# Attention values kept in the array and weights normalised on GpSimd: one change to a two-block transformer kernel

## What is computed

```
u    = rms_norm(x, norm_pre);  proj = u @ w_in
q_a, kv_a, g_a, z_a, qkv_b, z_b, merge = split(proj)
# attention a: 8 heads of 64, three branches, each gated per head and token
o_a  = g[0] * softmax(q_a kc) vc  +  g[1] * softmax(q_a ks) vs  +  g[2] * softmax(q_a kw) vw
y_a  = o_a * silu(z_a)
o_b  = softmax(q_b k_b) v_b            # attention b, 8 heads, no gate
y_b  = o_b * silu(z_b)
m    = sigmoid(gate_a) * (y_a @ w_a) + sigmoid(gate_b) * (y_b @ w_b)
x    = x + rms_norm(m @ w_o, norm_post)
```

## Time and profile before

| what | us |
|---|---|
| median of 3 runs | 634.45 |
| lowest and highest | 634.45, 637.77 |
| span of the profiled execution, first to last instruction | 632.1 |
| own time of the profiled execution | not listed apart from the runs; span and surroundings are taken as the median's 634.45, so 2.35 lie around the span |
| PE busy, 3510 matmul instructions | 568.5 |
| DVE busy, 701 instructions | 298.7 |
| ACT busy, 453 instructions | 213.9 |
| POOL busy, 68 instructions | 38.9 |
| DMA | 193.36 MB, mean 306 GB/s |

### The profile page before, as it was taken

One profiled execution on the slowest core, in us unless ns is written; L12 is line 12 of the kernel. 1 busy time (PEld: TensorE's weight loads), 2 busy tenths in 40 slices (PEclk: granted clock), 3 DMA queues, 4 the chain that ended last, 5 costly groups with the idle time before them and its releaser, 6 DMA issues.

```text
span 632.1 us, 8828 instructions
## 1 busy us (share of the span) xinstructions
PE 568.5 (90%) x3510; PEld 372.4 (59%) x3510; DVE 298.7 (47%) x701; ACT 213.9 (34%) x453; POOL 38.9 (6%) x68
## 2 busy tenths in 40 slices
PE   8999999999999999999998999999989765675685
PEld 7988977777867887868774444455443411321232
DVE  2556467675668977774747766234220100100002
ACT  3345443654523622665337754131110100100002
POOL 2000000000000000010004433000000000000000
PEclk9999999999999999999999999999999997897899
DMA  9984965659679887435658333768999999999994
GB/s 358 331 284 166 378 272 199 255 227 383 268 311 432 321 302 290 173 113 234 245 242 336 163 101 134 311 244 324 399 430 427 425 428 426 428 423 431 426 419 175
DMA packets 23069, 193.36 MB, mean 306 GB/s; under 512 B 4211, under 2 KB 5619, under 8 KB 11253
## 3 DMA queue, kind: packets, MB, share of 16 engines
q1 hardware_dynamic: 21732, 190.11, 75.4%
q0 software_dynamic: 288, 1.57, 0.6%
q10 hardware_dynamic: 1008, 1.12, 0.6%
HBM read 191.21 MB, written 1.06 MB: 304 GB/s over the span
## 4 chain that ended last, share of the span: by engine, by line
PE 65%; DMA 20%; DVE 6%; ACT 3%; SPq 2%; issue 1%; POOL 1%; ACTq 0%; POOLq 0%; DVEq 0%
PE bank L1240 27%; DMA ring<-in_stream 19%; PE bank L1904 6%; PE bank L1217 5%; PE bank L1228 5%; PE bank L1840 2%; PE bank L1286 2%; PE bank L1768 2%; PE bank L1703 2%; PE bank L1555 2%; PE bank L1826 2%; SPq L833 2%; PE bank L1616 1%; PE bank L1950 1%; PE bank L1662 1%
## 5 line engine op out<-in xcount | busy, mean ns | idle before, releaser
L1240 PE MATMUL bank<-weight_parts,u_parts 128*128 128x512 f32 (+1 forms) x384 | 116.5, 386 | 0.8 <-DVE weight_parts L2216 0.4
L1240 PEld LDWEIGHTS bank<-weight_parts,u_parts 128*128 128x128 f32 x384 | 69.9, 188 | 17.0 <-issue 2.7
L2216 DVE TENSOR_TENSOR weight_parts<-ring,weight_parts 128x1024 fp32r<-128x1024 f32 x56 | 66.5, 1222 | 23.9 <-ACT weight_parts L859 21.9
L859 ACT ACTIVATE weight_parts<-ring 128x1024 fp32r<-128x1024 f32 x56 | 57.2, 1055 | 14.5 <-PE bank L1240 14.1
L1240 PE MATMUL bank<-weight_parts,x_parts 128*128 128x512 f32 (+1 forms) x128 | 48.4, 378 | 0.0
L1240 PE MATMUL bank<-u_parts,weight_parts 128*128 128x256 f32 x192 | 36.5, 286 | 0.9 <-DVE weight_parts L2216 0.7
L1193 POOL TENSOR_TENSOR small<-small 128x1 f32<-128x1 f32 (+1 forms) x14 | 8.5, 608 | 417.8 <-DVE small L2649 200.0
L921 ACT ACTIVATE sp<-sp,small 128x128 f32<-128x128 f32 (+1 forms) x48 | 21.3, 444 | 32.0 <-DVE small L2125 32.0
L1240 PEld LDWEIGHTS bank<-u_parts,weight_parts 128*128 128x128 f32 x192 | 30.4, 191 | 2.4 <-issue 1.2
L1141 ACT ACTIVATE sp<-bank 128x512 f32<-128x512 f32 x4 | 2.4, 597 | 74.1 <-PE bank L1904 74.1
L2621 DVE SCALAR_TENSOR_TENSOR sp<-sp,bank 128x512 f32<-128x512 f32 x4 | 2.7, 685 | 52.2 <-ACT sp L1141 52.2
(11 more groups left out here) (367 smaller groups left out, 1064.1 us busy)
## 6 DMA issues: line engine op xcount, KB each, us to landing
ring<-in_stream SPq DMA_DIRECT2D x35, 2048.0 KB, 9.7
qk<-in_stream SPq DMA_DIRECT2D x9, 2048.0 KB, 12.5
parts<-in_stream SPq DMA_DIRECT2D x9, 2048.0 KB, 20.0
tabs<-in_stream SPq DMA_DIRECT2D x6, 2048.0 KB, 17.1
mo<-in_stream SPq DMA_DIRECT2D x5, 2048.0 KB, 26.9
vvc<-in_stream SPq DMA_DIRECT2D x5, 2048.0 KB, 30.0
ring<-in_stream SPq DMA_DIRECT2D x6, 1024.0 KB, 6.4
vvc<-in_vecs SPq DMA_DIRECT2D x12, 512.0 KB, 8.6
```

The lines of the kernel that those rows point to most:

```text
L859: ins = act.activation(dst, src, ACT.Copy, scale=scale)
L1240: ins = pe_.matmul(o, lhs(a, c, i), rhs(b, c, i), start=(c == 0 and n == 0), stop=(c == chunks - 1 and n == 2))
L2216: dve.tensor_tensor(quarter(low, name, q), quarter(slot(name), name, q), quarter(high, name, q).bitcast(F32), ALU.subtract).then_inc(split ...
```

## The change

- **POOL scales the weights p.** When a unit's exponentials are done, POOL takes `sums ** -1` (4 columns), for NSA and WIN multiplies by the gate (4 columns), and multiplies the unit's p in `sp` by them, four `tensor_scalar` of 128, 256, 128, 256 columns. `turn` on PE waits for that (`p_scaled`) in place of `exps`. The two DMA issues for the mask table stand between the units on POOL.
- **Value products turned.** p is now the moving operand, the values the stationary one: two matmuls of 256 and two of 128 columns, in pairs on half of the array's columns each. The output has features on partitions.
- **DVE's `unit_out`** becomes one operation of 128x256 (copy, add, or for MOBA the multiplication by silu(z_b), so the `yb` multiplication goes).
- **The groups `yaT0`, `yaT1`, `ybT0`, `ybT1` are gone.** ACT makes the high part of all 1024 columns in one operation, DVE the low part in one.
- **`za` and `zb` become `turned_products`** (48 matmuls of 256 columns in place of 24 of 512), and `cO` is computed turned, with as many matmuls as before.
- **`parts_product` goes by quarters**: for each quarter of the weights it does all outputs, and releases the quarter after them.

```
@@ DENSE @@
-         "cO0", "cO1", "gA00", "gA10", "yaT0", "gA01", "yaT1", "gA11", "modT0", "wa00", "ybT0",
-         "wa10", "ybT1", "wa01", "wa11", "gB00", "gB10", "cxT00", "cxT01", "cxT10", "cxT11",
+         "cO0", "cO1", "gA00", "gA10", "gA01", "gA11", "modT0", "wa00",
+         "wa10", "wa01", "wa11", "gB00", "gB10", "cxT00", "cxT01", "cxT10", "cxT11",
@@ schedule @@
-        if name == "cO1":
+        if name == "gA10":
             out.append(("ya", 0))
+        if name == "gA01":
+            out.append(("ya low", 0))
         if name == "gA11":
             out.append(("yb", 0))
+            out.append(("yb low", 0))
@@ ACT @@
+                elif kind in ("ya", "yb"):
+                    if kind == "ya":
+                        eng.wait_ge(ya_ready, 1)
+                    else:
+                        eng.wait_ge(outs, len(UNITS))
+                    high, full = ((yaT, oa), (ybT, ob))[kind == "yb"]
+                    copy(high, full, None, 0.5).then_inc(y_high, 1)
@@ POOL @@
+                    for u, (kind, j) in enumerate(UNITS):
+                        if u in (5, 7):
+                            i = (u - 5) // 2
+                            eng.wait_ge(masked, 6 + 2 * i)
+                            eng.dma_start(both[0][:, i::2], both[1][:, i::2]).then_inc(moba_table_in[i], 16)
+                        eng.wait_ge(exps, u + 1)
+                        pool.tensor_tensor(rc[:, u, :], sums[:, u, :], half[:, 3:4].to_broadcast([P, 4]), ALU.pow)\
+                            .then_inc(unit_recip_in, 1)
+                        eng.wait_ge(unit_recip_in, u + 1)
+                        if kind != MOBA:
+                            g0 = 8 * (kind + 1) + j
+                            pool.tensor_tensor(rc[:, u, :].rearrange("p (b q) -> p b q", b=2),
...
+                            eng.wait_ge(unit_recip_gated, u + 1)
+                        for b in range(2):
+                            for q in range(TOK):
+                                k = spn[:, u % 2, b, P * q:P + S * q]
+                                ins = pool.tensor_scalar(k, k, rc[:, u, 2 * b + q:2 * b + q + 1], None, ALU.mult)
+                        ins.then_inc(p_scaled, 1)
@@ PE, parts_product @@
-                for i, o in enumerate(outs_):
-                    for c in range(chunks):
-                        if not last and i == 0 and c % 2 == 0:
-                            eng.wait_ge(split_v, 4 * k + quarter + c // 2 + 1)
...
-                        if last and i == len(outs_) - 1 and c % 2 == 1 and c < chunks - 1:
-                            ins.then_inc(part_used, 1)
+                for c in range(0, chunks, 2):
+                    if not last:
+                        eng.wait_ge(split_v, 4 * k + quarter + c // 2 + 1)
+                    for i, o in enumerate(outs_):
+                        for d in (c, c + 1):
...
+                    if last and c < chunks - 2:
+                        ins.then_inc(part_used, 1)
@@ PE, turn and pv @@
-                    eng.wait_ge(exps, u + 1)
+                    eng.wait_ge(p_scaled, u + 1)
...
+                    for t, a in ((0, 0), (1, P)):
+                        for b in range(2):
+                            c = HD * b if typ != MOBA else HD * (2 * j + b)
+                            ins = pe_.matmul(VB[HD * b:HD * b + HD, a:S], v[:, t, c:c + HD],
+                                             ptn[:, u % 2, b, S * t:S * t + S - a], start=(t == 0), stop=(t == 1),
+                                             tile_position=(0, HD * b))
@@ DVE, unit_out, ya and the low parts @@
+                o = VB[:, 0:S]
+                if u == 8:
+                    kept(eng, "zb1")
+                if kind == NSA:
+                    ins = dve.tensor_copy(oa[:, j, :], o)
+                elif kind == WIN:
+                    ins = dve.tensor_tensor(oa[:, j, :], oa[:, j, :], o, ALU.add)
+                else:
+                    ins = dve.tensor_tensor(ob[:, j, :], zb[:, j, :], o, ALU.mult)
...
+                elif kind in ("ya low", "yb low"):
+                    which = kind[:2] == "yb"
+                    low, high, full = ((yalow, yaT, oa), (yblow, ybT, ob))[which]
+                    eng.wait_ge(y_high, 1 + which)
+                    dve.scalar_tensor_tensor(low, full, 0.5, high.bitcast(F32), ALU.mult, ALU.subtract).then_inc(y_low, 1)
```

More of the change, by code:

```diff
@@ L130 @@
 N_VEC = 16
-VEC_AFTER = {"wa10": [0], "ybT1": [1], "cxT11": [2, 3, 4, 5], "wb00": [6, 7], "mT00": [8, 9], "wo00": [10, 11, 12, 13], "cc0": [14, 15]}
+VEC_AFTER = {"wa00": [0], "wa10": [1], "cxT11": [2, 3, 4, 5], "wb00": [6, 7], "mT00": [8, 9], "wo00": [10, 11, 12, 13], "cc0": [14, 15]}
 VEC_LOADS = {"W9": [0, 1], "M7": [2, 3], "W11": [4, 5], "WO0": [6, 7, 8, 9], "C1": [10, 11], "WO1": [12, 13, 14, 15]}
@@ L1355, in dense @@
                     done(turned_products(name, "W1", 256 * i, i == 1), name)
[L1356 removed]
+                elif name[:2] in ("za", "zb"):
+                    i = int(name[2])
+                    begin(name)
+                    done(turned_products(name, {"za": "W6", "zb": "W7"}[name[:2]], 256 * i, i == 1), name)
+                elif name[:2] in ("va", "vb", "gA", "gB"):
                     t = int(name[2])
[L1358 removed]
+                    sl = {"va": "W2", "vb": "W5", "gA": "W8", "gB": "W10"}[name[:2]]
                     if name[:2] in ("gA", "gB") and name[3] == "1":
@@ L1417, in dense @@
                     if (t, h) == (0, 0):
-                        for i in range(2):
-                            kept(eng, f"y{name[1]}T{i}")
+                        eng.wait_ge(y_low, 1 + (name[1] == "b"))
                     begin(name)
@@ L1642, in _ @@
                         eng.wait_ge(outs, u)
-                    for b in range(2):
-                        c = HD * b if typ != MOBA else HD * (2 * j + b)
-                        o = VB[:, 128 * b:128 * b + 128]
-                        pr = ptn[:, u % 2, b, :]
-                        pe_.matmul(o[:, 0:64], pr[:, 0:P], v[:, 0, c:c + HD], start=True, stop=True)
-                        pe_.matmul(o[:, 64:128], pr[:, P:2 * P], v[:, 0, c:c + HD], start=True, stop=False)
-                        ins = pe_.matmul(o[:, 64:128], pr[:, 2 * P:3 * P], v[:, 1, c:c + HD], start=False, stop=True)
+                    for t, a in ((0, 0), (1, P)):
[4 more added lines that the diff above has]
+                                             tile_position=(0, HD * b))
                     ins.then_inc(pvs, 1)
@@ L2292, in _ @@
                         leave(dve.tensor_copy(ksw, D_(name)[:, :].rearrange("p (i s) -> p i s", i=2)), name)
-                    elif name in ("yaT0", "yaT1", "ybT0", "ybT1"):
-                        t = int(name[3])
-                        high, low = (yaT, yalow) if name[1] == "a" else (ybT, yblow)
-                        low_part(name, low[:, :, t * P:(t + 1) * P], high[:, :, t * P:(t + 1) * P])
                     elif name[:2] == "mT":
@@ L2744, in stream_of @@
         parts[f"OUT{i}"] = a["w_out_2"][0][out_rows, 512 * i:512 * i + 512]
+    parts["WA"] = parts["WA"][pair]
     flat = {n: chunks(p).reshape(P, -1) for n, p in parts.items()}
```

95 lines of the change are left out of this document (37 added, 58 removed).

## The result

The changed kernel takes 643.13 us (median, 642.09 to 643.64) beside 635.0 us for the kernel before on the same chip: a ratio of 1.0133 (95% interval 1.0112 to 1.0155). That is **slower** by the bound of 0.5% that the prediction set. In a second comparison it was 642.06 to 633.98, ratio 1.0135 (1.0119 to 1.0151). The prediction said 630.5, with 627.0 to 638.5 as its range.

What follows compares the result with a forecast made beforehand. PE's list bounds the first block, time won there before about 200 us reaching the end one for one. Load -0.3, value products -4.0, `z` +1.05, transposes -2.15, unit 11 +1.5: -3.9 from 634.45, predicted 630.5, range 627.0 to 638.5.

Steps and rivals of the forecast that it cites:

- rival 1: Attention: DVE's splits hold POOL up fully, PE waiting at units 0, 4, 6, 8, 10; +5.3 us, 639.7, slower; chance 0.17.
- So 4.2 us for a gated unit, 3.9 for MOBA: POOL's step between exponentials and turn: its length per unit, bounds 3.6 and 7.8 us, scaling taken as 2.8.
- Units 2 to 10 ... No wait: Attention turns: tightest is unit 8, with 4.55 us left for POOL's 3.9, so PE does not wait.
- two rows in which POOL met one VectorE instruction of 0.48 us: POOL rows beside DVE's multiplication: delays of 0.1 to 0.26 us, read as speaking against rival 1's full price.
- is used up: Unit 0: PE reaches the turn 1.1 us earlier through `qb0`, but p is scaled only at 57.6, so the gain goes.
- The +0.8 at unit 1: Unit 1's turn: p scaled at 66.8 where the turn stood at 66.03, so PE is 0.8 us later.
- Saving 0.4 per unit: Value products on PE: from 1.28 us to 0.89 per unit, saving 0.28 to 0.53; ten counted, -4.0 us.
- the `z` groups: `za`, `zb` turned on PE: 5.75 us in place of 5.49, +0.26 for each of four groups, +1.05 in sum.
- the load of 9.73 us: Weight load after unit 1's turn that ended PE's 0.8 us idle; expected to set when PE leaves, whatever came before.
- unit 11's wait: Unit 11's turn: p scaled at 166.9, so PE waits 1.5 us, +1.5 in the sum.
- 0.3 sooner: PE leaves the load of 9.73 us 0.3 us earlier, since the subtractions it follows end earlier; -0.3 in the sum.
- Rival 4: Loads around 190 to 205 us set the pace, so the gain doesn't reach the end: 634.4 us; chance 0.12.

Runs made afterwards that it cites:

- x3_filler: Changed kernel plus unread identity transposes on TensorE before its waits for GpSimd at units 0, 4, 6, 8 and 10: 636.65 us, ratio 1.0034 to the kernel before.
- x1_unscaled: Changed kernel without GpSimd's reciprocals, gates and scaling, the turn waiting for the exponentials again: 626.95 us, ratio 0.9884 to the kernel before.
- x2_one_input: Changed kernel with VectorE's low parts of W1 to W9 and WA made by one-input multiplies, not subtractions: 629.49 us, ratio 0.9944 to the kernel before.

## Why the prediction was wrong

What came is rival 1, given 0.17: 10.6 us of waits where its terms make 10.7. Against its +5.3 us stand two more things: a second loss of 6.0 that stood in no case, and 2.2 more of gain than its terms have. The time it gave, 639.7, was 3.4 us under the median.

- **The step that failed: GpSimd's price.** "So 4.2 us for a gated unit, 3.9 for MOBA" was nearly right for a GpSimd left alone: 4.4 and 4.2 us, the power 1.03 (I took 0.98), the gate 0.2, the scaling 2.99 (I took 2.8). "Units 2 to 10 ... No wait" then failed, since beside splits the scaling alone takes 5.0 to 6.4 at units 4, 6, 8 and 10 (6.3 at unit 8). The waits came at the units that rival 1 names: 2.92 and 2.84 us at units 8 and 10 (2.9 each in the rival), 1.05 and 1.07 at 4 and 6 (1.1 each), and none at unit 11, covered as it says.
- **Why I gave it 0.17.** I read the strength of the hindrance from two rows in which POOL met one VectorE instruction of 0.48 us with a pause behind it, and made a fraction of it. The quantity doesn't scale so. In a row of splits an instruction of POOL waits out the rest of one subtraction and, at unit 8, nearly all of the next: 2.70 us for work of 0.92. The Trainium skill (SBUF — State Buffer, "SBUF: two separate sides") had the rule that makes this rival the forecast, and the trace now agrees with it, by that row. A rule with a named mechanism, whose case no row of before shows, should not be outweighed by rows of a milder case.
- **A term that was missing: the clock.** 6.0 us in the profiled run, 6.3 by x3_filler. PE never idled over 1 us in this stretch before, so the rows I had taken could not show it. But the page before did, in its last slices, where PE idles for up to 3.5 us at a time:

```profile
PEclk9999999999999999999999999999999997897899
```

From 520 us on the mean granted clock is 0.87 there. Those rows were the place to look for what a wait of some 3 us costs beyond itself.

- **Unit 0 and 1.** That the gain of `qb0` "is used up" is shown: PE stood there 1.1 us earlier and waited 2.74. Of the 1.1 us of waits that I had put in `qb0`, only 0.7 are there (the fourth is at 302 us); that its gain is still 1.1 isn't explained by them. The +0.8 at unit 1 did not come; its p was ready at 65.76 and its turn began at 69.23, behind a group delayed by unit 0.
- **Value products.** "Saving 0.4 per unit" holds. In the timeline a turn of the changed kernel starts at 158.16, its value products at 158.96 and the next group at 159.76, 1.60 in all; before, the same turn at 158.19 and what follows at 160.18, 1.99. They are four and take 0.80, the lower end of my 0.76 to 1.01, but the transposes ahead are 0.09 longer to the next start. My sum took ten of them; without waits all twelve count.
- **The rest of the gain.** The transposes are gone, the `z` groups take 5.92 to 5.95 from start to start in place of 5.66, 0.27 more as priced; the load of 9.73 us ends no idle in the changed kernel, PE being late. Without GpSimd's step the span was 7.3 us shorter than before, against 5.4 in my sum before unit 11's wait: the two products more, and the first group's gain, which without the step is not eaten. The term that was mis-sized is the load: PE was to leave it "0.3 sooner". In x1_unscaled the load ended a wait of 0.48 at 77.71, in the kernel before one of 0.84 at 79.83, so PE left it 2.1 sooner. From there to the modulation behind `wa11` it gained 5.0, where the terms make 5.1.
- **Rival 4** can be ruled out: the modulation behind `wa11` stood 9.1 us late in the changed kernel and 7.1 early in x1_unscaled (185.33), the spans 9.3 more and 7.3 less. PE's list is passed on to the end one for one, as forecast.

The ledger of the profiled runs: -7.3 for all parts but GpSimd's step, +10.6 waits, +6.0 clock, in sum +9.3, which is the difference of the spans. What stays open is what decides, behind a wait of 2.5 to 2.9 us, whether the clock falls, and why by quarters is worth 1.7 us on the kernel before (0.95 to 2.3 by its interval) where the list of waits for splits falls by 0.4 only (1.1 to 0.7).

## What to carry to other kernels

Before work goes to GpSimd, list the VectorE instructions that will run beside it, and price it at their length, not at its own: a row of long VectorE instructions lets it in only between two, and sometimes not there. A step with 0.7 us of slack and 3 us of hindrance costs more than the wait where TensorE's clock falls behind it, as it did here behind waits of 2.7 to 2.9 us. VectorE itself did the step in 1.4 us, a third of GpSimd's time alone, in a pause that it had; and a change that frees buffers earlier has to be read for what it starts earlier, and beside whom.

## What the runs showed of the hardware

- GpSimd's scaling of 256 columns took 0.92 us alone, 1.3 to 1.9 beside one-input multiplies of 0.7 us with gaps (x2_one_input), 1.6 to 2.7 beside subtractions of 1.2 us in a row. VectorE hardly paid: four subtractions took 4.9 instead of 4.63 us. Beside VectorE's reads of PSUM GpSimd took its 0.92 (917 ns).
- From 40 to 205 us of the profiled runs PE's clock fell to its lower level behind 12 of 14 waits of 1.8 to 4.3 us, at 1.4 to 2.9 us each, and behind none of those of 0.9 to 1.5. What it had done before each fall was to idle; where transposes that nobody reads filled the idle time, it stayed at 1.00 (x3_filler). These counts hold for this stretch: in the kernel before, from 490 to 518 us, the clock stayed at 1.00 with waits of 1.6, 1.9 and 2.2 us in it.
- One unit's value products in pairs on halves of the array, two of 256 columns and two of 128, took 0.80 us, less than the 1.01 of two pairs of 256.
